# Fewer modulation blocks ahead of the first projection, and the two conditions on four column groups of TensorE

## The reference, cut to what matters

```python
for i in range(DEPTH):                                    # 2 layers
    mod_l = split(silu(c) @ w_mod[i] + b_mod[i], 6)       # w_mod[i]: 1024 x 6144, f32
    mod_c = split(silu(c_ctx) @ w_mod[i] + b_mod[i], 6)
    h_l = rms_norm(x, norm1_g[i]) * (1 + mod_l[1]) + mod_l[0]
    h_c = rms_norm(ctx, norm1_g[i]) * (1 + mod_c[1]) + mod_c[0]
    y_l, y_c = mixer(h_l, h_c)            # projections to q, k, v; attention; w_o
    x = x + mod_l[2] * y_l
    x = x + mod_l[5] * mlp(rms_norm(x, norm2_g[i]) * (1 + mod_l[4]) + mod_l[3])
    # the context likewise in layer 0
```

## Time and profile before

| | us |
|---|---|
| runs | 3043.46, 3048.42, 3054.18 |
| median of the runs | 3048.42 |
| span of the profiled execution | 3041.6 |
| TensorE busy in it | 2881.9 |
| first projection matmul of layer 0 at | 124.16 |
| attention of layer 0, from its first scores | 304.49 |
| first matmul of w_o in layer 0 in the chain | 487.51 |

### The profile page before, as it was taken

How to read it: one execution, slowest core, us unless ns; L and a number is a source line. 1 busy time by engine, 2 the same in 40 slices (tenths; PEclk the granted TensorE clock), 3 DMA queues, 4 the chain that set the end, 5 groups by cost and what they waited for, 6 DMA issues and landing times.

```text
span 3041.6 us, 45702 instructions
## 1 busy us (share of the span) xinstructions
PE 2881.9 (95%) x18805; PEld 2472.8 (81%) x18805; DVE 1776.0 (58%) x3448; ACT 1275.5 (42%) x2297; POOL 90.0 (3%) x141
## 2 busy tenths in 40 slices
PE   8999888999988999999999998999999999989998
PEld 3568446788877868999999976989999999768998
DVE  1464665545556465677654556766566546576764
ACT  1253443432235444445444433554454434335543
POOL 1000000000013130000000000000000000000000
PEclk9999999999999999999999987999999999699999
DMA  8532333232243323456665430446666554114564
GB/s 278 175 114 81 125 115 107 69 97 97 97 110 85 103 23 110 156 181 168 175 184 151 130 100 23 153 126 184 176 181 169 174 157 145 55 62 155 139 168 124
DMA packets 503839, 397.16 MB, mean 131 GB/s; under 512 B 13656, under 2 KB 478816, under 8 KB 503504
## 3 DMA queue, kind: packets, MB, share of 16 engines
q1 hardware_dynamic: 499808, 385.00, 41.6%
q0 software_dynamic: 3104, 5.63, 1.6%
q10 hardware_dynamic: 720, 3.61, 0.3%
HBM read 393.15 MB, written 1.05 MB: 130 GB/s over the span
## 4 chain that ended last, share of the span: by engine, by line
PE 86%; DVE 8%; ACT 4%; DMA 1%; issue 1%; POOL 0%; SPq 0%; DVEq 0%; ACTq 0%
PE pv L614 39%; PE pa L614 29%; PE pv L577 11%; PE pa L577 5%; DVE Wl L1514 2%; ACT Wh L1107 2%; PE pa L582 1%; DMA ring<-in_w_mod_dram 1%; DVE Lb L1653 0%; ACT Pb L1192 0%; DVE T L1572 0%; DVE T L1571 0%; DVE TMP L1584 0%; DVE HTl L1591 0%; DVE TMP L1606 0%
## 5 line engine op out<-in xcount | busy, mean ns | idle before, releaser
L1514 DVE TENSOR_TENSOR Wl<-ring,Wh 128x1024 fp32r<-128x1024 f32 (+3 forms) x688 | 758.9, 1145 | 375.4 <-ACT Wh L1107 373.0
L1107 ACT ACTIVATE Wh<-ring 128x1024 fp32r<-128x1024 f32 (+3 forms) x688 | 646.8, 990 | 525.6 <-PE pv L614 506.6
L614 PE MATMUL pa<-HTl,Wh 128*128 128x256 f32 (+1 forms) x1648 | 537.0, 326 | 49.3 <-DVE HTl L1591 29.3
L614 PE MATMUL pv<-HTl,Wh 128*128 128x256 f32 (+1 forms) x1872 | 548.4, 293 | 9.0 <-DVE XT L1631 2.2
L614 PE MATMUL pv<-HTh,Wl 128*128 128x256 f32 (+1 forms) x1872 | 538.7, 288 | 0.0
L614 PE MATMUL pv<-HTh,Wh 128*128 128x256 f32 (+1 forms) x1872 | 538.2, 287 | 0.0
L614 PE MATMUL pa<-HTh,Wl 128*128 128x256 f32 (+1 forms) x1648 | 524.7, 318 | 0.0
L614 PE MATMUL pa<-HTh,Wh 128*128 128x256 f32 (+1 forms) x1648 | 524.5, 318 | 0.0
L614 PEld LDWEIGHTS pa<-HTl,Wh 128*128 128x128 f32 x1648 | 324.5, 197 | 78.5 <-issue 47.1
L614 PEld LDWEIGHTS pv<-HTl,Wh 128*128 128x128 f32 x1872 | 360.7, 193 | 24.5 <-issue 9.5
L614 PEld LDWEIGHTS pv<-HTh,Wl 128*128 128x128 f32 x1872 | 361.0, 193 | 3.2 <-issue 0.5
(11 more groups left out here) (216 smaller groups left out, 4325.5 us busy)
## 6 DMA issues: line engine op xcount, KB each, us to landing
ring<-in_ffn_w_gu_dram SPq DMA_DIRECT2D x176, 512.0 KB, 5.1
ring<-in_w_mlp_dram SPq DMA_DIRECT2D x64, 1024.0 KB, 5.2
ring<-in_w_in_dram SPq DMA_DIRECT2D x54, 1024.0 KB, 5.2
ring<-in_w_mod_dram SPq DMA_DIRECT2D x48, 1024.0 KB, 5.3
ring<-in_ffn_w_down_dram SPq DMA_DIRECT2D x64, 704.0 KB, 4.6
ring<-in_a_w_qkv_dram SPq DMA_DIRECT2D x12, 1024.0 KB, 6.2
ring<-in_b_w_qkv_dram SPq DMA_DIRECT2D x12, 1024.0 KB, 5.2
ring<-in_w_out_dram SPq DMA_DIRECT2D x8, 1024.0 KB, 5.0
```

Source lines behind the costliest of these rows:

```text
L614: m = nc.tensor.matmul(o, lhsT=x, rhs=y, start=first and j == 0, stop=last and j == 2)
L1107: ins = nc.scalar.activation(Wh[0:rows, p % SPLIT, a:b], ring[0:rows, i % RING, a:b], ACT.Copy)
L1514: ins = v.tensor_tensor(Wl[0:rows, p % SPLIT, a:b], ring[0:rows, i % RING, a:b], Wh[0:rows, p % SPLIT, a:b].bitcast(F32), ALU.subtract)
```

## The change

Only eight blocks, the shift and the scale of layer 0's norm 1, stay ahead of the first projection (`FIRST_MOD`). The other 40 (`LATER_MOD`) are taken in order, 16 of layer 0 and 24 of layer 1: 20 in the projections, one behind every tile j and one behind each value block, and 20 in the attention, in the same steps as before. The list of weights has two modulation blocks behind each q/k block and one behind each value block. The gains of norm 2 of layer 0 are made behind the attention.

`cT` is now 32 columns wide for each of the eight tiles, zero but for two, and lies in BIG; GpSimd clears it at the start. The eight matmuls of a block write 32 partitions each of one bank, tile k on column group k % 4, so that each group sums two tiles. The 128x256 result is copied whole, and instead of a transpose a matmul with the constant `fold` (128x2, ones where p % 32 is 0 or 1) adds the four groups and turns the row into columns. ACT issues the token and constant loads at the very start.

```diff
...
-QK_MOD = 4
-X_AFTER = N_MOD * D // 512
+FIRST_MOD = 2 * D // 256
+LATER_MOD = DEPTH * MOD_BLOCKS - FIRST_MOD
+QK_MOD = 20
+X_AFTER = 2
...
+    put("fold", (p[:, None] % 32 == np.arange(2)[None, :]) * 1.0)
...
-    return n if QK_MOD <= n <= MOD_BLOCKS else None
+    return n if QK_MOD <= n <= LATER_MOD else None
+def later_modulation(m):
+    return divmod(FIRST_MOD + m, MOD_BLOCKS)
...
-        modrow = BIG[0:2, 5120:5120 + N_MOD * D]
-        modtwo = BIG[0:2, 12288:12800].rearrange("p (b n) -> p b n", n=256)
+        modrow = big(5120, FIRST_MOD, 256)
+        modtwo = big(12288, 2, 256)
+        cT = big(12800, KT, 32)
...
+        def columns_of_modulation(m):
+            layer, n = later_modulation(m)
+            return I["w_mod"][layer], n * 256
...
             if i == 0:
-                by_columns(I["w_mod"][0], 0, N_MOD * D, 256, False)
-                for n in range(QK_MOD):
-                    by_columns(w, n * 512, (n + 1) * 512)
-                    columns(I["w_mod"][1], n * 256, 256, False)
-                by_columns(w, 2 * D, 3 * D)
-                by_columns(I["w_mod"][1], QK_MOD * 256, N_MOD * D, 256, False)
+                by_columns(I["w_mod"][0], 0, FIRST_MOD * 256, 256, False)
+                later = [columns_of_modulation(m) for m in range(LATER_MOD)]
+                for n in range(8):
+                    by_columns(w, n * 256, (n + 1) * 256)
+                    for src, c in later[2 * n:2 * n + 2]:
+                        columns(src, c, 256, False)
+                for n in range(8, 12):
+                    by_columns(w, n * 256, (n + 1) * 256)
+                    columns(*later[8 + n], 256, False)
+                for src, c in later[QK_MOD:]:
+                    columns(src, c, 256, False)
...
-            def used(pool, key):
-                done[state["block"] - 1] = (pool.full, pool.nth(key))
+            def used(pool, key, block=None):
+                done[state["block"] - 1 if block is None else block] = (pool.full, pool.nth(key))
...
+            def condition_rows(pool, key):
+
+                w = raw_slot()
+                if pool.taken():
+                    pe.wait_ge(pool.free, pool.taken())
+                b = pool.take(key)
+                for k in range(KT):
+                    j = k % 4
+                    m = nc.tensor.matmul(b[32 * j:32 * j + 32, 0:256], lhsT=cT[:, k, :], rhs=w[:, k, :],
+                                         start=k < 4, stop=k >= 4)
+                m.then_inc(pool.full, 1)
+                used(pool, key)
...
                 pe.wait_ge(v_free, V.nth("cond"))
-                for n in range(MOD_BLOCKS):
-                    w = raw_slot()
-                    group(V, ("modr", i, n), lambda b: b[0:2, 0:256], [(cT[:, k, :], w[:, k, :], None) for k in range(KT)])
-                    used(V, ("modr", i, n))
+                for n in range(FIRST_MOD):
+                    condition_rows(V, ("modr", i, n))
                     if n == X_AFTER:
+                        pe.wait_ge(const_in, 16)
...
                         turn_in("x", xtok, 4)
-                    if n == X_AFTER + 5:
-                        pe.wait_ge(const_in, 16)
+                    if n == X_AFTER + 3:
...
                 b = V.take(("mod", i))
-                pe.wait_ge(v_free, V.nth(("modr", i, MOD_BLOCKS - 1)))
-                for n in range(N_MOD * KT):
-                    m = nc.tensor.transpose(b[:, 2 * n:2 * n + 2], modrow[:, n * P:(n + 1) * P], C("ident")[0:2, 0:2])
-                m.then_inc(v_full, 1)
+                pe.wait_ge(v_free, V.nth(("modr", i, FIRST_MOD - 1)))
+                for n in range(2 * KT):
+                    mm(b[:, 2 * n:2 * n + 2], modrow[:, n // 2, n % 2 * P:n % 2 * P + P], C("fold"), True, True,
+                       v_full if n == 2 * KT - 1 else None)
...
-                if n < MOD_BLOCKS:
-                    w = raw_slot()
-                    group(A, ("modr", 1, n), lambda b: b[0:2, 0:256], [(cT[:, k, :], w[:, k, :], None) for k in range(KT)])
-                    used(A, ("modr", 1, n))
+                if n < LATER_MOD:
+                    condition_rows(A, ("modr", n))
                 if n:
-                    pe.wait_ge(a_free, A.nth(("modr", 1, n - 1)))
+                    pe.wait_ge(a_free, A.nth(("modr", n - 1)))
...
                         pe.wait_ge(a_free, A.taken())
-                    b = A.take(("modt", 1, n - 1))
+                    b = A.take(("modt", n - 1))
                     for j in range(2):
-                        m = nc.tensor.transpose(b[:, 2 * j:2 * j + 2], modtwo[:, (n - 1) % 2, j * P:(j + 1) * P],
-                                                C("ident")[0:2, 0:2])
-                    m.then_inc(a_full, 1)
+                        mm(b[:, 2 * j:2 * j + 2], modtwo[:, (n - 1) % 2, j * P:(j + 1) * P], C("fold"), True, True,
+                           a_full if j else None)
...
                         group(V, ("qr", i, j - 2), lambda b: b[:, 0:S], [(C("pairs"), tiles[j - 2][0][:, LAT], None)])
-                    if i == 0 and j < order and j % 4 == 3:
-                        next_modulation(j // 4)
+                    if i == 0:
+                        next_modulation(j)
...
                     tokens_major(A, ("v", i, n), split_slot(), CTX_TOKS + LAT_TOKS)
+                    if i == 0:
+                        next_modulation(order + n)
...
-                if n < MOD_BLOCKS:
-                    copy(("modr", 1, n), modtwo[:, n % 2, :], lambda b: b[0:2, 0:256])
+                if n < LATER_MOD:
+                    copy(("modr", n), modtwo[:, n % 2, :], lambda b: b[:, 0:256])
                 if n:
-                    act.wait_ge(a_full, A.nth(("modt", 1, n - 1)))
-                    b = A.bank(("modt", 1, n - 1))
+                    act.wait_ge(a_full, A.nth(("modt", n - 1)))
+                    b = A.bank(("modt", n - 1))
+                    layer, block = later_modulation(n - 1)
                     for j in range(2):
-                        t = 2 * (n - 1) + j
-                        ins = nc.scalar.activation(MOD[:, 1, t, :], b[:, 2 * j:2 * j + 2], ACT.Identity,
-                                                   bias=col("bmod", N_MOD * KT + t))
+                        t = 2 * block + j
+                        ins = nc.scalar.activation(MOD[:, layer, t, :], b[:, 2 * j:2 * j + 2], ACT.Identity,
+                                                   bias=col("bmod", layer * N_MOD * KT + t))
...
                         inverse_root(RQ[:, (j - 1) % 2, 0:n], XQ[:, (j - 1) % 2, 0:n], b[:, 0:n], HEAD)
-                    if i == 0 and j % 4 == 3:
-                        next_modulation(j // 4)
+                    if i == 0 and j < len(tiles):
+                        next_modulation(j)
...
                         prepare()
+                    if i == 0:
+                        next_modulation(len(tiles) + n)
...
+            src = [I[x][0].rearrange("(t p) d -> p t d", p=P) for x in ("ctx", "x")]
+            for t in range(4):
+                nc.scalar.dma_start(xtok[:, t, :], src[t // 2][:, t % 2, :]).then_inc(tok_in, 16)
+            nc.scalar.dma_start(con[:, P:], I["pack"][:, P:]).then_inc(const_in, 16)
...
+            act.wait_ge(c_zero, 1)
...
-            for j in range(5):
-                act.wait_ge(v_full, V.nth(("modr", 0, 2 * j)))
-                if j == 0:
-                    nc.scalar.dma_start(con[:, P:], I["pack"][:, P:]).then_inc(const_in, 16)
-                else:
-                    src = I["ctx" if j <= 2 else "x"][0].rearrange("(t p) d -> p t d", p=P)
-                    nc.scalar.dma_start(xtok[:, j - 1, :], src[:, (j - 1) % 2, :]).then_inc(tok_in, 16)
...
-                for n in range(MOD_BLOCKS):
-                    copy_in(("modr", 0, n), modrow[:, n * 256:(n + 1) * 256], lambda b: b[0:2, 0:256])
+                for n in range(FIRST_MOD):
+                    copy_in(("modr", 0, n), modrow[:, n, :], lambda b: b[:, 0:256])
...
-                    if n == X_AFTER + 7:
+                    if n == X_AFTER + 4:
...
-                n = N_MOD * KT
-                v.tensor_tensor(MOD[:, 0, :, 0], b[:, 0:2 * n:2], col("bmod", 0, n), ALU.add)
-                v.tensor_tensor(MOD[:, 0, :, 1], b[:, 1:2 * n:2], col("bmod", 0, n), ALU.add).then_inc(v_free, 1)
+                n = 2 * KT
+                v.tensor_tensor(MOD[:, 0, 0:n, 0], b[:, 0:2 * n:2], col("bmod", 0, n), ALU.add)
+                v.tensor_tensor(MOD[:, 0, 0:n, 1], b[:, 1:2 * n:2], col("bmod", 0, n), ALU.add).then_inc(v_free, 1)
...
-            def gains(i):
-                for which, (name, at) in enumerate((("norm1", 1), ("norm2", 4))):
+            def gains(i, *norms):
+                for which in norms:
+                    name, at = (("norm1", 1), ("norm2", 4))[which]
...
+                    gains(0, 0)
...
-                    dve.wait_ge(a_free, A.nth(("modt", 1, MOD_BLOCKS - 1)))
-                gains(i)
+                    gains(1, 0, 1)
```

(13 more changed lines are left out.)

## The result

The kernel after takes 3069.55 us (median of four runs, 3064.4 to 3071.92), the kernel before, on the same chip, 3046.78: a ratio of 1.0069, 95% interval 1.0052 to 1.0085. It is slower by 0.7%. The profiled execution has a span of 3068.3 us, against 3041.6 before.

What follows compares the result with a forecast made beforehand. TensorE, busy 95% of the span, was taken to bound the kernel. Lead -62, projections +82, clock +16, attention -27 and +6, gains +0.5 sum to +15.5; on the 3048.4 median that gives 3064 us, range 3045 to 3085.

Steps and rivals of the forecast that it cites:

- One block: A modulation block on TensorE: four column groups side by side, 1.07 us plus a 0.45 fold, 1.52 for 3.75.
- Rivals 2: Modulation blocks: column groups do not overlap, 3.54 us a block stays and folds are extra; 3139 us, chance 0.09.
- Rival 3: Modulation blocks: matmuls in strict order, 2.14 us a block; +40, 3088 us, chance 0.13.
- The nine slots: A modulation block under strict order: a tile's second instruction keeps the next group back, 9 slots instead of 4.
- The lead: Up to the first projection matmul: blocks removed, transfers now bound it, first matmul at 62 us, -62 (bounds -65 to -54).
- The projections without the clock: Layer 0's projections: late qkv loads make TensorE wait, 24.9 to 25.3 us a pair of tiles, 263 for 180.3, +82.
- The circle of the forecast: One pair in the projections: late load, ACT's split and root, VectorE's gain, TensorE's rotation, blocks and tile, then the load again.
- The clock: Layer 0's projections: eight halts of TensorE, each followed by half clock, 8 x 2 = +16 us (0 to 24).
- the price of a halt: Half clock after TensorE idles: 2.5 us, read from the first 45 tile matmuls of the projections, taken at 2.
- The attention: Layer 0's attention: shorter blocks take 45 us off TensorE, -27 for the stage, and clock dips add +6 (0 to 25).
- The share of six tenths: Layer 0's attention: the part of the 45 us taken off TensorE that shortens the stage, giving -27.
- Rival 1: Layer 0's projections: qkv loads get in before ACT's prepare, so no such wait; -66, 2982 us, chance 0.10.

Runs made afterwards that it cites:

- e8: The changed kernel with qkv loads a pair earlier, and ACT's five token and constant loads issued only when modulation block 0 has landed: 2972.2 us.
- e1: The changed kernel with each qkv block's load one pair earlier in SP's list, nothing else moved: 2974.6 us, ratio 0.9762 to the kernel before.
- e5: The changed kernel with ACT's and VectorE's split of the qkv block put behind the tile's root, newton and modulation copies, in layer 0 alone: 3007.6 us.
- e3: The changed kernel without column groups: all eight tiles of a modulation block summed in the first group of 32 rows: 3163.1 us, ratio 1.0382.
- e10: e1 with the twenty modulation blocks in layer 0's attention left out, with their loads, folds and copies: 2949.6 us, ratio 0.9688.
- e6: The changed kernel with the edits of e1 and e5 together: 2967.8 us, ratio 0.9736 to the kernel before.
- e4: The changed kernel's column groups, folds and early ACT loads, but with the blocks not moved, in the old list and steps: 3012.0 us, ratio 0.9886.

## Why the prediction was right, and where its sizes were off

The direction, the mechanism and the time hold: 3064 was forecast, 3069.6 measured, in the forecast's own range of 3045 to 3085. By the spans the sum was further off: +15.5 forecast, +26.7 measured. Of these 11 us, 6 don't show in the time, because the 6.8 us that were added for the difference of span and median belong to the spread of the executions: each profiled run stands only 1.9 us above its span (3043.46 and 3070.2). That part of the closeness is luck. Step by step, with the signs of the sum:

- **One block**: 1.07 + 0.45 = 1.52 was taken. The chain has 1.00 to 1.05 for the block and 0.54 for the fold at full clock. TensorE's order of time shows the overlap that the earlier trace rows only suggested. It gives, at one block, four instructions in the time of one:

```profile
76.53 0.42 PE L744 MATMUL pa<-ring,BIG 128*32 128x256 f32 x4
...
76.53 1.07 PE L744 MATMUL pa<-ring,BIG 128*32 128x256 f32 x16
```

3.54 us became 1.0, a factor of 3.5. Rivals 2 (3.54) and 3 (2.14) fall with these rows. Rival 3's order, matmuls strictly one behind the other in their starts and ends, is what the Trainium skill gives (TensorE: Matmul & The Clock Gate, Part 3: Packing small matmuls), with 2.38x for three groups. The nine slots were my reading of that order for matmuls of two instructions, and the trace doesn't show them: no tile's second instruction keeps the next group back. The page's factor is for three groups, so the 3.5 for four neither bears it out nor contradicts it.

- **The lead**, -62: measured -60.7. The three first blocks were to be in at 23, and were at 26.1; the norm sums ended at 44.1 (41.7), block 11 was asked for at 50.8 (49) and landed at 56.5 (55). The last path, from that load through the split to the first matmul, was foretold, and each step came some 2 us late. I had not foreseen that SP's three blocks, asked for at 2 to 3.4 us, would all come in behind ACT's 3.6 MB; by e8 this costs about 1 us in the end.

- **The projections without the clock**, +82, a pair at 24.9 to 25.3. The circle of the forecast is the chain of the trace: SP's two issues, the load (8.25 and measured 7.9 to 9.3), the split, the root, VectorE's 3.0 us. PE's wait for the root was to be 6.5 us and is 6.2 (37.3 in six). At the first pair modt was to stand behind ACT's prepare, and does: 12.1 us, once. (The forecast's own terms add up to 24.75 us a pair and 262 for the stage, where it says 24.9 and 263; nothing hangs on it.) e1 removes the circle and the stage falls to 193, 12.7 above before for the +15 of the blocks' own work; e5 leaves the load late and takes away only what stood behind it: both halves of the claim are shown.

- **The clock**, +16 of 0 to 24: this term failed. By e1's stage with the same instructions it was 32.9 us, twice as much. The step that failed is the price of a halt, 2.5 us and taken at 2, read from the first tiles of the projections; that half-clock stretch ran from 118.4 to 128.7, and more than half of it had passed when they began at 124.16. The number of halts, eight, was right. In the kernel after each is followed by a stretch at half clock, seven of 10 to 17 us and one of 7. TensorE is busy for 63 us in the eight, so half of that, 4 us a halt, is what half clock adds: to the rotation, two blocks and folds, and in most pairs to the tile (up to 2.6 us). With it the pairs last 29.0 us (five from 111.97 to 256.89), not 27. What idle time cost was a little less than forecast: 279 was to be 195 of work, 68 of idle, 16 of clock, and was 193, 63 and 33.

- **The attention**, -27 and +6 for the clock, -21: measured -20.7. The share of six tenths was a guess between 0 and 1. e3's 0.59 and e10's 0.68 look like it, but both have the clock in them, as the measured -20.7 has, and that is less than half of the 45. TensorE was busy for 125.6 us, not the 110 of the forecast, with a granted clock of 0.85 against 0.95: it worked 41 us at half clock, against 11 before, and half of the 30 us between them is the difference of 15. How much of these 15 us lengthened the stage is not shown, so neither the -27 nor the +6 is; that their sum came out within 0.3 us is in part luck.

- **Rival 1**, loads that get ahead, would have decided under 21.7 us a pair. In the trace a pair takes 27 to 31 us. Its time, 2982, is close to e1's 2974.6: the kernel it described exists, with each qkv load two entries further up the list.

Not settled: how much of the clock in the attention the shorter blocks cause and what it costs there, what bounds the lead of e1, and whether e6 is faster than e1.

## What to carry to other kernels

When work is put between the consumers of a ring of buffers, write down, for each load, whose release frees its slot and at which instruction the in-order engine waits for it; loads that stood one place too late in the list cost 80 us here, with the DMA engines two thirds idle. Ask also what is queued behind the wait: moving one engine's wait behind work that was ready won 61 us in a stage whose loads were still late, and the same edit cost 14 to 17 us in a layer that had no such wait. And price a halt of TensorE at full: its idle time, and what it then does at half clock, which in this stage came to 33 us on 63 of idle time.

## What the runs showed that was not expected

The granted clock in the lead's rows is 1.00 while modulation blocks take 2.0 us there (0.43 us from one set of four matmuls to the next), twice what they take at 76.5 us, also under clock 1.00:

```profile
26.51 1.98 PE pv L748 x16
```

That is e1's third block; its records name a clock event only from 29.4 us on, at 1.00, and blocks from 34 us on take their 1.0. In e4 it lasts longer: thirteen blocks take 2.0 us each up to 58.3 us, with 1.00 in the column all the while, and its first clock event is at 60 us. So at the start of a trace, up to the first clock event, the pace of the matmuls says more of the clock than the clock's column.

Transfers of two queues, issued in the same two microseconds, did not share evenly: ACT's five loads were in at 5.3 to 15.2 us, SP's three blocks at 20.5, 23.3 and 26.1, though SP had issued the first two before ACT's fifth. In e8, where ACT issued only when block 0 had landed, at 7.1, SP's third block, issued at 3.0, still landed only at 22.1. Why is not shown.
